# LayerNorm statistics on VectorE, sample states loaded by eight, other DMA estimates in the planner, and a reordered end, in an eight-core hybrid decoder step

## The reference

```python
def layer_forward(x, p, s_hgrn, s_conv, ...):
    xn = rmsnorm(x, norm_mix_w)
    z = xn @ w_in                                   # 1024 -> 5120
    q_pre, f_pre, i_in, og, u_pre, v_pre, g_a, g_b = jnp.split(z, ...)
    # branch A: gated recurrence, per head a 128 x 128 state, in chunks of 64
    fg = lb + (1.0 - lb) * sigmoid(f_pre)
    o_rec, s_new = hgrn2_recurrence(silu(q_pre), 1 - fg, i_in, log(fg), s_hgrn)
    o_a = rmsnorm(o_rec * sigmoid(og), hgrn_norm_w)
    # branch B: spatial gate inside chunks of 128 positions
    u = gelu(u_pre)
    v = layernorm(gelu(v_pre), ln_v_w, ln_v_b)      # over 512 columns
    o_b = u * (tril(W_s) v + b)                     # per chunk, 4 channel groups
    mix = (sigmoid(g_a) * (o_a @ w_a_out) + sigmoid(g_b) * (o_b @ w_b_out)) @ w_o
    h = x + mix
    # ConvFFN: up 1024 -> 2 x 2816, causal width-3 conv, gelu(a) * b, down 2816 -> 1024
    h = h + conv_ffn(rmsnorm(h, norm_ffn_w), ...)
    # per-layer embedding (PLE)
    return h + sigmoid(rmsnorm(h, norm_ple_w) @ w_ple_gate) * (p @ w_ple_proj)
y = rmsnorm(h, final_norm_w)
```

## Time and profile before

| | us |
|---|---|
| median of 3 runs | 1122.34 (1122.22 to 1124.01) |
| the profiled execution | 1124.0 |
| its span on core 2, the slowest | 1122.5 |
| its spans on the other cores | 1112.2 to 1121.2 |
| PE busy in the span | 1044.7 (93%) |
| DVE, ACT, POOL busy | 655.8, 587.7, 447.2 |

### The profile page before, as it was taken

How to read it: one execution, slowest core, us unless ns; L and a number is a source line. 1 busy time by engine, 2 the same in 40 slices (tenths; PEclk the granted TensorE clock), 3 DMA queues, 4 the chain that set the end, 5 groups by cost and what they waited for, 6 DMA issues and landing times.

```text
span 1122.5 us, 20148 instructions; the slowest of 8 cores (1112.2 to 1122.5 us)
## 1 busy us (share of the span) xinstructions
PE 1044.7 (93%) x5658; PEld 495.9 (44%) x5658; DVE 655.8 (58%) x1054; ACT 587.7 (52%) x1147; POOL 447.2 (40%) x648
## 2 busy tenths in 40 slices
PE   5968998798899899999999999999999999999993
PEld 1433463343444344554444444555444444444441
DVE  2537646573355564553788888999898333333332
ACT  3678777786433332231567766888766222222221
POOL 1043432645333634332453353655533333333332
PEclk9979999999899899999999999999999999999997
DMA  9924154159956677872892123850566456553311
GB/s 192 182 91 145 60 175 136 72 120 199 189 197 226 152 236 157 179 254 42 206 190 77 42 73 76 148 127 20 143 196 178 133 150 175 132 169 99 99 57 47
DMA packets 84012, 155.51 MB, mean 139 GB/s; under 512 B 41536, under 2 KB 48448, under 8 KB 80576
## 3 DMA queue, kind: packets, MB, share of 16 engines
q1 hardware_dynamic: 74832, 118.51, 33.8%
q0 software_dynamic: 9072, 35.72, 19.9%
HBM read 129.91 MB, written 51.10 MB: 161 GB/s over the span
## 4 chain that ended last, share of the span: by engine, by line
PE 74%; DMA 12%; POOL 4%; DVE 3%; issue 3%; ACT 2%; SPq 0%; POOLq 0%; DVEq 0%; ACTq 0%
PE bank L576 73%; POOL arena L533 3%; DMA arena<-xpT 3%; DMA arena<-w_in 3%; DMA arena<-st_h 2%; DMA arena<-arena 2%; DVE arena L533 2%; ACT arena L525 1%; DVE arena L548 1%; PE bank L574 1%; DMA o_hs<-arena 1%; DMA d_ob<-arena 1%; DMA arena<-c_late 1%; ACT L525 0%; SPq L499 0%
## 5 line engine op out<-in xcount | busy, mean ns | idle before, releaser
L576 PE MATMUL bank<-arena 128*128 128x512 bf16 (+2 forms) x5334 | 1030.5, 355 | 39.4 <-ACT arena L525 20.9
L576 PEld LDWEIGHTS bank<-arena 128*128 128x128 bf16 (+1 forms) x5334 | 478.9, 99 | 577.0 <-issue 84.0
L533 POOL TENSOR_TENSOR arena<-arena 128x1 f32<-128x1 f32 (+8 forms) x464 | 375.1, 816 | 401.1 <-DVE arena L548 215.3
L525 ACT ACTIVATE arena<-arena 128x512 f32<-128x512 f32 (+6 forms) x349 | 234.6, 692 | 226.2 <-POOL arena L533 63.8
L548 DVE SCALAR_TENSOR_TENSOR arena<-bank,arena 128x511 f32<-128x511 f32 (+3 forms) x502 | 316.8, 658 | 60.7 <-ACT arena L525 19.5
L525 ACT ACTIVATE arena<-bank,arena 128x512 f32<-128x512 f32 (+1 forms) x264 | 183.7, 703 | 143.8 <-PE bank L576 142.0
L525 ACT ACTIVATE arena<-bank 128x2 f32<-128x2 f32 (+5 forms) x419 | 148.5, 365 | 148.1 <-PE bank L576 112.9
L533 DVE TENSOR_TENSOR arena<-arena,bank 128x512 f32<-128x512 f32 (+1 forms) x121 | 79.1, 659 | 144.9 <-PE bank L576 106.3
L548 DVE SCALAR_TENSOR_TENSOR arena<-arena 128x512 bf16<-128x512 f32 (+5 forms) x114 | 100.7, 903 | 79.3 <-ACT arena L525 60.1
L548 DVE SCALAR_TENSOR_TENSOR arena<-arena,bank 128x512 f32<-128x512 f32 (+2 forms) x108 | 70.3, 655 | 100.8 <-ACT arena L525 73.9
L540 POOL TENSOR_SCALAR arena<-arena 128x1 f32<-128x1 f32 x68 | 20.7, 305 | 108.8 <-ACT arena L525 108.4
(11 more groups left out here) (21 smaller groups left out, 57.3 us busy)
## 6 DMA issues: line engine op xcount, KB each, us to landing
arena<-w_up POOLq DMA_DIRECT2D x22, 512.0 KB, 9.6
d_g<-arena SPq DMA_DIRECT2D x20, 512.0 KB, 3.1
arena<-d_g SPq DMA_DIRECT2D x20, 512.0 KB, 7.0
arena<-xpT SPq DMA_DIRECT2D x16, 512.0 KB, 8.2
arena<-w_in POOLq DMA_DIRECT2D x8, 1024.0 KB, 17.7
arena<-xp SPq DMA_DIRECT2D x16, 512.0 KB, 7.5
d_h<-arena SPq DMA_DIRECT2D x16, 512.0 KB, 5.5
arena<-d_h SPq DMA_DIRECT2D x16, 512.0 KB, 5.2
```

The lines of the kernel that those rows point to most:

```text
L525: return self.g.op("act", lambda e: e.activation(out=_rv(out), in_=_rv(in_), func=func, **kw), reads, writes, dur, tset=TSET.get(func))
L533: return self.g.op(eng, lambda e: e.tensor_tensor(out=_rv(out), in0=_rv(a), in1=_rv(b), op=op), reads, writes, dur)
L576: r = e.matmul(_rv(out), l, rh, start=st, stop=sp)
```

## The change

Five edits:

1. **Planner.** `DMA_BW` 305 to 330, `DMA_LAT` 800 to 1600, and a transfer's bytes count times (1 + 600 / packet size). No instruction changes by this, but every engine's order may.
2. **LayerNorm statistics of v** (17 tiles). Before: Gelu with a running sum, a Square with a running sum, six small GpSimd operations, an Identity with scale and bias, where ScalarE did the three large ones. After: Gelu, `bn_stats` and `bn_aggr` on VectorE, two small GpSimd operations, and (v - mean) * rstd as a TENSOR_SCALAR on VectorE.
3. **The copy to `kh`** of the prompt units (16) goes from ScalarE to VectorE.
4. **Sample states** by eight sequences: 8 loads and 8 stores of 512 KB in place of 16 and 16 of 256 KB, in 4 buffers of double size; the compute stays by four.
5. **The end of 2b.** `h` and `hf_` are tracked by halves. The PLE part of the next-to-last tile is given a later priority (24), and the last tile's end is done by halves: its adds into `h` on VectorE, a square sum per half, h * weight early, and the last scaling by one half on ScalarE and one on VectorE, with two stores of 256 KB.

```diff
-DMA_BW = 305.0
+DMA_BW = 330.0
-DMA_LAT = 800.0
+DMA_LAT = 1600.0
-                o.left = float(o.dma)
+                o.left = float(o.dma) * (1.0 + 600.0 / o.pkt)
+    def gmlp_stats(vg):
+        st = pST.new()
+        E.bn(st[:, 0:6], vg.ap, [vg], [st])
+        ms = pST.new()
+        E.bn_aggr(ms[:, 0:2], st[:, 0:6], [st], [ms])
+        E.ts(ms[:, 1:2], ms[:, 1:2], EPS, None, ALU.add, None, [ms], [ms], eng="pool")
+        E.tt(ms[:, 1:2], ms[:, 1:2], negh[:, 0:1], ALU.pow, [ms, negh], [ms], eng="pool")
+        return ms
-            E.act(kh.ap, p.b(0, 512), AF.Copy, [p], [kh])
+            E.cp(kh.ap, p.b(0, 512), [p], [kh], rate=1.8)
-            E.act(vg.ap, p.f(), AF.Gelu, [p], [vg, st], accum=st[:, 0:1])
+            E.act(vg.ap, p.f(), AF.Gelu, [p], [vg])
-            E.act(vn.ap, vg.ap, AF.Square, [vg], [vn, st], accum=st[:, 4:5], psum=False)
-            st3 = gmlp_stats(st, 1)
-            E.act(vn.ap, vg.ap, AF.Identity, [vg, st3], [vn], scale=st3[:, 0:1], bias=st3[:, 4:5], psum=False)
+            ms = gmlp_stats(vg)
+            E.ts(vn.ap, vg.ap, ms[:, 0:1], ms[:, 1:2], ALU.subtract, ALU.mult, [vg, ms], [vn], rate=1.6)
...
-        pS0 = LS_.pool(512, F32, 7); pS0B = LS_.pool(512, BF16, 4); pVB = LS_.pool(512, BF16, 2)
+        pS0 = LS_.pool(1024, F32, 4, nsub=2); pS0B = LS_.pool(1024, BF16, 2, nsub=2); pVB = LS_.pool(512, BF16, 2)
+            for c2 in range(2):
+                s0 = pS0.new()
+                seqs = slice(c2 * 8, (c2 + 1) * 8)
+                E.load(s0.ap, st_h[h, :, seqs, :].rearrange("p j v -> p (j v)"), [s0], 524288)
+                for k in range(2):
+                    ...
+                    if k == 1:
+                        E.store(o_hs[h, :, seqs, :].rearrange("p j v -> p (j v)"), s0.ap, [s0], 524288)
...
+        g.prio_shift = late
         for hf in range(2):
             ...
-            E.tt(h[:, hs], h[:, hs], tg.ap, ALU.add, [h, tg], [h], eng="pool")
+            E.tt(h[:, hs], h[:, hs], tg.ap, ALU.add, [(h, hf), tg], [(h, hf)], eng="dve" if last else "pool")
+            if last:
+                E.act(hf_[:, hs], h[:, hs], AF.Square, [(h, hf)], [(hf_, hf), (st, 2 + hf)],
+                      accum=st[:, 2 + hf:3 + hf], scale=float(D) ** -0.5, psum=False)
+                E.tt(hf_[:, hs], h[:, hs], fnw[:, hs], ALU.mult, [(h, hf), fnw], [(hf_, hf)])
+        g.prio_shift = 0
+        if last:
+            E.ts(st[:, 4:5], st[:, 2:3], st[:, 3:4], EPS, ALU.add, ALU.add, [(st, 2), (st, 3)], [(st, 4)], eng="pool")
+            E.tt(st[:, 4:5], st[:, 4:5], negh[:, 0:1], ALU.pow, [(st, 4), negh], [(st, 4)], eng="pool")
+            E.act(hf_[:, 0:512], hf_[:, 0:512], AF.Copy, [(hf_, 0), (st, 4)], [(hf_, 0)], scale=st[:, 4:5], psum=False)
+            E.store(y[:, 0:512], hf_[:, 0:512], [(hf_, 0)], P * D * 2)
+            E.ts(hf_[:, 512:1024], hf_[:, 512:1024], st[:, 4:5], None, ALU.mult, None, [(hf_, 1), (st, 4)], [(hf_, 1)],
+                 rate=2.0)
+            E.store(y[:, 512:1024], hf_[:, 512:1024], [(hf_, 1)], P * D * 2)
+            return
...
-            tile_2b(u, i, gt)
+            tile_2b(u, i, gt, 24 if (u, i) == (NQ - 1, 2) else 0, (u, i) == (NQ - 1, 3))
```

66 lines of the change are left out of this document (28 added, 38 removed).

## The result

| | before | after |
|---|---|---|
| median, us | 1123.17 (1122.22 to 1125.18, 4 runs) | 1095.2 (1093.9 to 1095.7, 4 runs) |
| ratio to before | | 0.9747, 95% interval 0.9729 to 0.9764 |
| profiled execution, span of the slowest core | 1122.5 (core 2) | 1094.1 (core 3) |
| spans of all cores | 1112.2 to 1122.5, mean 1116.9 | 1088.0 to 1094.1, mean 1091.4 |
| TensorE busy in the slowest span | 1044.7 (93%) | 1034.2 (95%) |

The kernel became 2.5% faster, 28 us. The forecast was 1105, 17 us; the time lies inside the range of 1093 to 1117, nearer to the rival "the clock comes back" (1091) than to the forecast. In the two profiled executions the mean of the cores fell by 25.5 us, and the slowest core stands 2.7 us above that mean in place of 5.6.

A forecast was written before the change was run, and what follows sets the result against it. TensorE's idle time in 56 to 400 us and at the end, with low clock behind pauses, was taken as the loss; 9.5 (order in 1a) + 4 (states) + 3.4 (end) = 17 us gave 1105, range 1093 to 1117.

The forecast's parts named there:

- the clock comes back: Rival, chance 0.16: fewer pauses in 56 to 336 us also take the low clock with them; 32 us gained, 1091.
- What bounds the kernel, and that 400 to 880 us can't be won: TensorE is busy 477.55 of 480 us there at full clock; the idle time lies in 56 to 400 us and the end.
- The loads of the helpers: In 56 to 280 us ScalarE falls to near 35 and VectorE rises to near 39 us of 56.
- Unit 3 and the start of 1b: More matmuls cover the recurrence before unit 3's outputs, 4 us (0 to 7); Tanhs go before a state copy, 1.5 us.
- Units 1, s and 2: Stage 1a, 9.7 us idle in small pieces in 168 to 224 us: 2 us gained (-3 to 6).
- Unit 0: Recurrence can start earlier, but VectorE's eight norm products of unit 1 stand ahead of two steps: 2 us gained (-3 to 6).
- Sample states: Waits in 336 to 400 us for reused buffers, 8.4 us in all: half goes, 4 us gained (-2 to 8).
- covered on average and not where DMA is slow: Sample states: 16 us of TensorE work stand against store and load of 13 us plus 3.2 us, so half is taken.
- The end: TensorE done 6 us earlier, but the next-to-last tile's tail precedes the last's on ScalarE and VectorE: 3.4 us gained.
- Slower: Rival, chance 0.05: VectorE becomes the late engine of the recurrence, four units pay 23 us; 1136.
- adds more than 2.5 us apart: Sign that the forecast is wrong: recurrence adds in stage 1a this far apart, against 2.14 us a chunk before.

## Why the prediction was right, and where it fell short

- **What bounds the kernel, and that 400 to 880 us can't be won:** right for stages 1b and 2a. The sum had no term for the short waits for transposes in stage 2b, 0.9 us as a mean and 1.3 on the slowest core, which I hadn't looked for behind 880 us.
- **The loads of the helpers:** expected near 35 (ScalarE) and 39 us of 56 (VectorE) in 56 to 280; measured 37.5 and 41.3 as means of the four stretches. The groups of the changed kernel in 56 to 300 us (count, busy us, mean ns):

```profile
L542 DVE TENSOR_SCALAR arena<-arena 128x512 bf16<-128x512 f32 x16 | 15.0, 936 | 3.8 <-POOL arena L533 3.8
...
L558 DVE BATCH_NORM_STATS2 arena<-arena 128x6 f32<-128x512 f32 x17 | 11.5, 683 | 6.6 <-ACT arena L525 6.5
...
L554 DVE COPY arena<-bank 128x512 bf16<-128x512 bf16 x12 | 5.0, 415 | 1.3 <-PE bank L591 1.3
...
L561 DVE BATCH_NORM_AGGREGATE arena<-arena 128x2 f32<-128x6 f32 x17 | 3.0, 176 | 0.7
```

  `bn_stats` at 0.683 (I took 0.69), `bn_aggr` at 0.176 (0.15) and the copy at 0.415 (0.59) were near; the scaling took 0.94 in place of 0.59 (see the last section).
- **Unit 3 and the start of 1b:** 5.5 us expected, 8.5 measured on the slowest cores (11.8 to 3.3). The mechanism was the one forecast (cover grows from 32 to 64 matmuls). "I take 4 us gained (0 to 7)" counted the 5.84 us of the wait alone, less inserts. Of the 8.5, 6.1 are idle time: the wait of 5.84 and the one of 1.85 at the start of 1b went, and a new one of 1.98 came; the forecast's 5.5 is near that. The other 2.4 are the 4.74 us at half clock behind the long wait. I had written that idle time costs again behind itself, and then priced the wait without it. The table of outputs above shows the first of that price: 3.2 to 3.6 us where the long wait is, 2.0 to 2.2 where it isn't (2.8 on two cores, with a pause inside).
- **Units 1, s and 2, the term that was mis-sized most:** 2 us expected. Up to 210 us 4.8 are won on the mean core (10.0 to 5.2) and 3.5 on the slowest, and to where unit 3 begins another 3.9 and 3.1: around unit 2's outputs the longest pause went from 1.45 us to 0.41, and of 5.3 us at half clock 3.4 are left (slowest cores). The forecast had the 9.7 us idle in 168 to 224 and took a fifth of them, with no row for which would go. The part up to 210 comes with edit 2: every kernel without edits 2 and 3 stays at 8.9 to 10.0, and with edit 2 and the copy on ScalarE it is 3.6.
- **Unit 0:** 2 us expected, none measured (34.4 and 35.1). The fear named there came true: the eight norm products of unit 1 stand ahead of a recurrence step, and TensorE waits for them. VectorE, then TensorE:

```profile
74.36 5.84 DVE L548 SCALAR_TENSOR_TENSOR arena<-arena 128x512 bf16<-128x512 f32 x8 [0.59 <-ACT arena L525]
80.12 0.68 DVE L533 TENSOR_TENSOR arena<-arena,bank 128x512 f32<-128x512 f32 x1
```

```profile
80.45 3.57 PE L583 MATMUL bank<-arena 128*128 128x512 bf16 x8 [6.14 <-DVE arena L548]
```

- **Sample states:** 4 us expected, 4.4 on the mean core, 7.9 on the slowest. The step "covered on average and not where DMA is slow" was wrong in its second half: no core loses over 2.1 us now. The longest wait of ScalarE for a state is 2.5 us, 8.5 in all. The slowest core had the most to win here. I had read that difference between cores 2 and 3 off and not put it into the sum, which is made on the slowest core. The 3.2 us that the prediction took for a 512 KB transfer from the Trainium skill's "DMA: Bandwidth & Descriptors", section "Anatomy of one DMA", is there a fit for GpSimd's path, and the states go by SP's queue: their loads landed after 6.3 us and their stores after 7.4 (medians).
- **The end:** 3.4 us expected. From the last cast to the last scaling I had 16.4 us, measured 1088.53 - 1071.71 = 16.8, in the way forecast (the next-to-last tile in front on both engines), with no pause on TensorE ahead of the last gate. The span then ended 5.6 us behind the last scaling, with two stores of 256 KB, where it was 7.0 with one of 512 KB, so 4.3 + 22.5 - 22.4 = 4.4 us in all on the slowest cores.
- **Sum, on the slowest cores:**

| | forecast | measured |
|---|---|---|
| to 145 us (unit 0 and the start) | 2 | -1.4 |
| to 247 us of before (units 1, s, 2) | 2 | 6.6 |
| to 311 us of before (unit 3, start of 1b) | 5.5 | 8.5 |
| to 400 us (states) | 4 | 7.9 |
| stages 2a and 2b up to the last cast, without the moved matmuls | 0 | 1.9 |
| the end | 3.4 | 4.4 |
| together | 17 | 27.9 of 28.4 |

The missing 0.5 lies between 400 us and the end of stage 1b. Five terms were too small and the first had the wrong sign, four of them by 3 us or more; that the range held (its lower end is 1093, the time 1095.2) owes something to luck.

- **The rivals:** "the clock comes back" was right in what it said of the clock (busy time at 1.2 GHz up to 400 us: 33 us on the slowest core before, 19 after) and said half would go. "Slower", with VectorE late in the recurrence, was right that each step becomes longer. Its sign, adds more than 2.5 us apart, came in unit 1: 2.53 to 2.55 us a step on every core, 2.06 before; in unit 3 it is 2.39 to 2.57. It did not make the kernel slower, since unit 3's recurrence starts 14.6 us earlier and has more matmuls beside it.
